# Two blocks instead of one in six attention steps: where a transformer kernel computes the gates of its merge

## The reference, cut to what matters

```
h = rmsnorm(x, norm_g)
a_b, a_c, a_x, a_z, c_q, c_kv, k_pe, b_z, dq, dk, dv, c_z, gate_pre = split(h @ w_in)

u = a_c * a_x                                  # branch a: a convolution over 3 tokens
conv = conv_b + sum(shift(u, tap) * conv_w[tap] for tap in range(3))
y_a = a_b * conv * silu(a_z)
y_b = causal_attention(q, k, v) * silu(b_z)    # branch b: 8 heads (MLA)
y_c = dilated_attention(dq, dk, dv) * silu(c_z)  # branch c: 8 heads, 3 dilations each

g_a, g_b, g_c = split(sigmoid(gate_pre + b_gate))
merged = g_a * (y_a @ w_out_a) + g_b * (y_b @ w_out_b) + g_c * (y_c @ w_out_c)
return x + merged @ w_o
```

## Time and profile before

| | us |
|---|---|
| median of 3 runs | 1566.07 |
| lowest and highest run | 1561.93, 1566.72 |
| the profiled execution, its own time | 1560.04 |
| its span, first to last instruction | 1558.2 |
| TensorE busy | 1503.1 |
| VectorE busy | 1025.5 |
| ScalarE busy | 854.6 |
| GpSimd busy | 83.9 |
| mean granted TensorE clock | 0.993 |

### The profile page before, as it was taken

How to read it: one execution, slowest core, us unless ns; L and a number is a source line. 1 busy time by engine, 2 the same in 40 slices (tenths; PEclk the granted TensorE clock), 3 DMA queues, 4 the chain that set the end, 5 groups by cost and what they waited for, 6 DMA issues and landing times.

```text
span 1558.2 us, 31924 instructions
## 1 busy us (share of the span) xinstructions
PE 1503.1 (96%) x11856; PEld 1411.6 (91%) x11856; DVE 1025.5 (66%) x1774; ACT 854.6 (55%) x1433; POOL 83.9 (5%) x136
## 2 busy tenths in 40 slices
PE   8988999999999999999999999899999999989998
PEld 7777999999989899999999988789999898878998
DVE  2787788898955556555467647775646664776664
ACT  3446566544445646664466755554446675655453
POOL 0111000111000000000000000310000000031000
PEclk9999999999999999999999999999999999999999
DMA  9775488898663355666463553226546355413663
GB/s 375 265 259 183 150 299 290 287 386 315 234 206 119 95 186 165 192 195 191 149 222 123 161 178 123 69 96 189 187 153 206 120 168 171 142 55 98 197 194 122
DMA packets 81341, 292.78 MB, mean 188 GB/s; under 512 B 9200, under 2 KB 10480, under 8 KB 81088
## 3 DMA queue, kind: packets, MB, share of 16 engines
q1 hardware_dynamic: 67408, 244.03, 47.7%
q0 software_dynamic: 11792, 42.83, 8.0%
q10 hardware_dynamic: 2016, 4.21, 0.8%
HBM read 289.99 MB, written 1.05 MB: 187 GB/s over the span
## 4 chain that ended last, share of the span: by engine, by line
PE 47%; issue 40%; DVE 6%; ACT 3%; POOL 2%; DMA 1%; SPq 0%; POOLq 0%; DVEq 0%; ACTq 0%
PE G L450 12%; PE G L451 12%; PE G L452 12%; POOL bias L426 2%; DVE wlo L1374 2%; DVE aw L1382 1%; ACT whi L968 1%; PE S L531 1%; PE G L476 1%; PE G L478 1%; PE G L477 1%; PE Tp L758 1%; PE G L496 1%; PE G L502 1%; PE Tp L557 0%
## 5 line engine op out<-in xcount | busy, mean ns | idle before, releaser
L1374 DVE TENSOR_TENSOR wlo<-raw,whi 128x1024 fp32r<-128x1024 f32 x444 | 541.9, 1223 | 317.0 <-ACT whi L968 310.8
L450 PE MATMUL G<-h,whi 128*128 128x256 f32 x2192 | 626.2, 286 | 5.5 <-DVE cz L1825 3.6
L451 PE MATMUL G<-h,whi 128*128 128x256 f32 x2192 | 610.9, 279 | 0.0
L452 PE MATMUL G<-h,wlo 128*128 128x256 f32 x2192 | 610.6, 279 | 0.0
L968 ACT ACTIVATE whi<-raw 128x1024 fp32r<-128x1024 f32 x444 | 468.9, 1058 | 232.6 <-PE G L452 180.2
L450 PEld LDWEIGHTS G<-h,whi 128*128 128x128 f32 x2192 | 415.8, 190 | 15.7 <-issue 12.1
L451 PEld LDWEIGHTS G<-h,whi 128*128 128x128 f32 x2192 | 414.5, 189 | 1.8 <-issue 0.5
L452 PEld LDWEIGHTS G<-h,wlo 128*128 128x128 f32 x2192 | 414.0, 189 | 0.0
L1382 DVE CUSTOM_DVE_ANT_0 aw<-aw,cs,cols 128x1024 f32<-128x1024 f32 x80 | 102.3, 1278 | 0.0
L450 PE MATMUL G<-ah,whi 128*128 128x256 f32 x352 | 97.2, 276 | 0.0
L451 PE MATMUL G<-ah,whi 128*128 128x256 f32 x352 | 97.2, 276 | 0.0
(11 more groups left out here) (290 smaller groups left out, 2300.9 us busy)
## 6 DMA issues: line engine op xcount, KB each, us to landing
raw<-in_w SPq DMA_DIRECT2D x444, 512.0 KB, 4.1
aw<-in_ada POOLq DMA_DIRECT2D x80, 512.0 KB, 5.1
adaw<-in_ada SPq DMA_DIRECT2D x8, 1024.0 KB, 17.8
sn<-in_uq ACTq DMA_DIRECT2D x2, 768.0 KB, 6.9
x<-in_x SPq DMA_DIRECT2D x1, 1024.0 KB, 5.5
pt<-in_ukv ACTq DMA_DIRECT2D x2, 512.0 KB, 8.5
out<-x SPq DMA_DIRECT2D x4, 256.0 KB, 2.4
dist<-in_dist POOLq DMA_DIRECT2D x1, 576.0 KB, 4.1
```

What stands on the lines that cost most here:

```text
L450: pe.matmul(o, wh, mv[:, 0:T], start=(k == 0), stop=False)
L451: pe.matmul(o, wh, mv[:, T:2 * T], start=False, stop=False)
L452: ins = pe.matmul(o, wl, mv[:, 0:T], start=False, stop=(k == k_of - 1))
L1374: dve.tensor_tensor(wlo[:, s, :], raw[:, s, :], whi[:, s, :], ALU.subtract).then_inc(w_lo, 1)
```

## The change

Six gate blocks a layer, those of mm = 1 (`EARLY`), leave the merge. Each of the steps 9 to 14 gets one, behind its convolution block. A table `WHAT` now says of every block beside the heads what it is ("z", "conv" or "gate") and its number; a table `MERGE` gives the first block and tile of each round of the merge, and the rounds of mm = 1 consist of their `w_out` block alone. ScalarE takes the tanh of an early gate tile in `head_block` and puts it in `sq` instead of `th`, where it stays until VectorE multiplies by it in mm = 1. VectorE does nothing for a gate block in the steps but `next_lo`. Blocks, tiles, instructions and bytes are the same in number; the weights are laid out in the new order.

```diff
-H_MERGE = 64
+H_MERGE = 70
...
-for _n in range(H_MERGE - H_CZ):
-    BESIDE[0 if _n < 3 else _n - 2 if _n < 18 else 16].append(H_CZ + _n)
+WHAT = {}
+EARLY = 1
+for _n in range(20):
+    _i = 0 if _n < 3 else _n - 2 if _n < 18 else 16
+    for _w in [("z", _n) if _n < 4 else ("conv", _n - 4)] + ([("gate", _i - 9)] if 9 <= _i < 15 else []):
+        WHAT[H_CZ + len(WHAT)] = _w
+        BESIDE[_i].append(H_CZ + len(WHAT) - 1)
+assert len(WHAT) == H_MERGE - H_CZ
+
+
+MERGE = {}
+_b = _g = H_MERGE
+for _n in range(12):
+    MERGE[_n // 3, _n % 3] = (_b, _g)
+    _b, _g = (_b + 1, _g + 2) if _n // 3 == EARLY else (_b + 3, _g + 4)
+H_WO_TILE = _g
...
-                        bb, n = B_HYB + H_MERGE + 9 * mm + 3 * r, G_HYB + H_MERGE + 12 * mm + 4 * r
-                        run(bb, n, 1, 8, of_h, b4=b4, g4=g4)
-                        if mm == 0 and r == 0:
-                            pair_outs(7)
-                        run(bb + 1, n + 1, 1, 8, of_h, b4=b4, g4=g4)
-                        if mm == 0 and r == 0:
-                            pe.wait_ge(y_lo, l * 12 + 12)
-                        run(bb + 2, n + 2, 2, 4, lambda m, k: yh[:, 4 * ((2 * r + m) % 3) + k, :], b4=b4, g4=g4,
+                        bb, n = B_HYB + MERGE[mm, r][0], G_HYB + MERGE[mm, r][1]
+                        if mm != EARLY:
+                            run(bb, n, 1, 8, of_h, b4=b4, g4=g4)
+                            if mm == 0 and r == 0:
+                                pair_outs(7)
+                            run(bb + 1, n + 1, 1, 8, of_h, b4=b4, g4=g4)
+                            if mm == 0 and r == 0:
+                                pe.wait_ge(y_lo, l * 12 + 12)
+                            bb, n = bb + 2, n + 2
+                        run(bb, n, 2, 4, lambda m, k: yh[:, 4 * ((2 * r + m) % 3) + k, :], b4=b4, g4=g4,
                             half=half_done)
...
+                def gate_tanh(dst, mm, pair, n):
+
+                    col = 8 * (pair % 3) + 2 * mm + pair // 3
+                    freed(act.activation(dst[:, pair, :], gslot(G_HYB + n), ACT.Tanh, scale=0.5,
+                                         bias=hb[:, col:col + 1]), n)
+
                 def head_block(j):
                     done(j)
-                    t, kind = (j - H_A) // 4, (j - H_A) % 4
-                    if j < H_A:
-                        act.activation(cz[:, j - H_CZ, :], gslot(G_HYB + j), ACT.Tanh, scale=0.5).then_inc(tanh_ready, 1)
+                    what, n = WHAT[j]
+                    t, kind = n // 4, n % 4
+                    if what == "z":
+                        act.activation(cz[:, n, :], gslot(G_HYB + j), ACT.Tanh, scale=0.5).then_inc(tanh_ready, 1)
+                    elif what == "gate":
+                        gate_tanh(sq, EARLY, n, j)
...
+                def merged(m):
+                    act.wait_ge(m_ready, l * 8 + m + 1)
+                    act.activation(mh[:, m, 0:T], mg[:, m % 2, :], ACT.Copy, scale=0.5).then_inc(m_hi, 1)
+
                 for mm in range(4):
-                    for q in range(9):
-                        j = H_MERGE + 9 * mm + q
+                    for r in range(3):
+                        j, n = MERGE[mm, r]
+                        for q in range(0 if mm == EARLY else 2):
+                            done(j)
+                            gate_tanh(th, mm, 2 * r + q, n + q)
+                            next_hi(j)
+                            if r == 2 and q == 0:
+                                merged(2 * mm)
+                            j += 1
                         done(j)
-                        if q % 3 < 2:
-                            pair = 2 * (q // 3) + q % 3
-                            n = H_MERGE + 12 * mm + 4 * (q // 3) + q % 3
-                            col = 8 * (pair % 3) + 2 * mm + pair // 3
-                            freed(act.activation(th[:, pair, :], gslot(G_HYB + n), ACT.Tanh, scale=0.5,
-                                                 bias=hb[:, col:col + 1]), n)
                         next_hi(j)
-                        if q in (6, 8):
-                            m = 2 * mm + q // 8
-                            act.wait_ge(m_ready, l * 8 + m + 1)
-                            act.activation(mh[:, m, 0:T], mg[:, m % 2, :], ACT.Copy, scale=0.5).then_inc(m_hi, 1)
+                        if r == 1 and mm == EARLY:
+                            merged(2 * mm)
+                    merged(2 * mm + 1)
...
-                    if j < H_A:
-                        dve.wait_ge(tanh_ready, l * 12 + (4 + j - H_CZ + 1))
-                        freed(dve.scalar_tensor_tensor(out=cz[:, j - H_CZ, :], in0=cz[:, j - H_CZ, :], scalar=1.0,
+                    what, t = WHAT[j]
+                    if what == "z":
+                        dve.wait_ge(tanh_ready, l * 12 + (4 + t + 1))
+                        freed(dve.scalar_tensor_tensor(out=cz[:, t, :], in0=cz[:, t, :], scalar=1.0,
                                                        in1=gslot(n), op0=ALU.add, op1=ALU.mult), j)
+                    if what != "conv":
                         next_lo(j)
                         return
...
-                        bb = H_MERGE + 9 * mm + 3 * r
-                        gate = G_HYB + H_MERGE + 12 * mm + 4 * r + q % 2
-                        n = gate + 2
+                        bb, n = MERGE[mm, r][0], G_HYB + MERGE[mm, r][1] + q % 2
                         m = 2 * mm + q // 3
-                        next_lo(bb + q % 2)
+                        if mm == EARLY:
+                            gate, tg = G_HYB + [j for j in WHAT if WHAT[j] == ("gate", q)][0], sq
+                        else:
+                            gate, tg = n, th
+                            next_lo(bb + q % 2)
+                            bb, n = bb + 2, n + 2
                         if q % 2:
-                            done(bb + 2)
+                            done(bb)
                         else:
                             dve.wait_ge(half_done, l * 12 + 3 * mm + r + 1)
                         dve.wait_ge(slot_free[gate % 4], taken(gate) + g4)
...
-                            freed(dve.scalar_tensor_tensor(out=th[:, q, :], in0=th[:, q, :], scalar=1.0, in1=gslot(n),
+                            freed(dve.scalar_tensor_tensor(out=tg[:, q, :], in0=tg[:, q, :], scalar=1.0, in1=gslot(n),
                                                            op0=ALU.add, op1=ALU.mult), n - G_HYB)
...
-                            next_lo(bb + 2)
+                            next_lo(bb)
```

More of the change, by code:

```diff
@@ L1332, in _ @@
                         for j in TAKEN[i]:
-                            if j >= H_A and (j - H_A) % 4 == 3:
-                                t = (j - H_A) // 4
+                            if WHAT[j][0] == "conv" and WHAT[j][1] % 4 == 3:
+                                t = WHAT[j][1] // 4
                                 y_split(t, (a_ready, l * 4 + t + 1), at[:, 3, :])
@@ L1822, in head_block @@
                     n = G_HYB + j
-                    if j < H_A:
-                        dve.wait_ge(tanh_ready, l * 12 + (4 + j - H_CZ + 1))
-                        freed(dve.scalar_tensor_tensor(out=cz[:, j - H_CZ, :], in0=cz[:, j - H_CZ, :], scalar=1.0,
+                    what, t = WHAT[j]
+                    if what == "z":
+                        dve.wait_ge(tanh_ready, l * 12 + (4 + t + 1))
+                        freed(dve.scalar_tensor_tensor(out=cz[:, t, :], in0=cz[:, t, :], scalar=1.0,
                                                        in1=gslot(n), op0=ALU.add, op1=ALU.mult), j)
+                    if what != "conv":
                         next_lo(j)
                         return
-                    t, kind = (j - H_A) // 4, (j - H_A) % 4
+                    t, kind = t // 4, t % 4
                     if kind == 1:
@@ L1871, in _ @@
                         for j in TAKEN[i]:
-                            if j >= H_A and (j - H_A) % 4 == 3:
-                                y_split((j - H_A) // 4, at[:, 3, :])
+                            if WHAT[j][0] == "conv" and WHAT[j][1] % 4 == 3:
+                                y_split(WHAT[j][1] // 4, at[:, 3, :])
                     if i >= 3 and i % 2:
@@ L1891, in _ @@
                         if q % 3 == 0:
-                            freed(dve.scalar_tensor_tensor(out=mg[:, m % 2, :], in0=th[:, q, :], scalar=1.0, in1=gslot(n),
+                            freed(dve.scalar_tensor_tensor(out=mg[:, m % 2, :], in0=tg[:, q, :], scalar=1.0, in1=gslot(n),
                                                            op0=ALU.add, op1=ALU.mult), n - G_HYB)
                         else:
-                            freed(dve.scalar_tensor_tensor(out=th[:, q, :], in0=th[:, q, :], scalar=1.0, in1=gslot(n),
+                            freed(dve.scalar_tensor_tensor(out=tg[:, q, :], in0=tg[:, q, :], scalar=1.0, in1=gslot(n),
                                                            op0=ALU.add, op1=ALU.mult), n - G_HYB)
```

(12 more changed lines are left out.)

4 lines of the change are left out of this document (2 added, 2 removed).

## The result

The changed kernel takes 1596.24 us (median of 4 runs, 1594.04 to 1609.03), the kernel before in the same measurement 1566.05 us (4 runs, 1561.93 to 1566.72): a ratio of 1.0201, 95% interval 1.0163 to 1.0239. In a second measurement it was 1600.03 against 1567.35 us, 1.0191 (1.0147 to 1.0235). So it is slower by about 30 us; 1592 was predicted.

The account below looks back on a forecast made before the run. TensorE, busy 1503 of 1558 us, was taken as the bound. Per layer, steps +24.1, merge -15.7 and clock +5.1 gave +13.5, both layers +27.0 us: 1592 us, range 1574 to 1608.

Parts of the forecast that it names:

- The tile wait: Steps 9 to 14: blocks wait for a G tile VectorE frees late; new idling 16.1 us a layer.
- Step 9: First step with an added block: its gate block waits for step 8's kind-2 tile; length 10.8 us, +1.7 on 9.04.
- The steps in sum: Steps 9 to 14 together: +24.1 us a layer for work and waits, before the clock's +5.1.
- The clock: Slow starts of TensorE behind the idles of steps 10, 12 and 14: 1.7 us each, +5.1 us a layer.
- HAM oscillation: Skill section on repeating waits that each drop the clock: all three idles of both layers start slow; without it 10.2 us less.
- the rival in which the clock stays up: Steps 9 to 14: the wait is there without slow starts, 5.1 us a layer less, 1583 us; chance 0.2.
- Step 15: Step behind the six changed ones: keeps its blocks, has no late tile, adds 0.
- My cover for the lo: Steps 9 to 14: VectorE's added lo (1.22 us a step) costs nothing; if cover failed, 7 us a layer.
- The merge: Six gate blocks fewer save 16.9 us a layer, dense mm = 1 rounds give back 1.2: -15.7 a layer.
- The first rival: Steps 9 to 14: added blocks simply fill TensorE's idle time, -15 us in all, 1551 us; chance 0.05.

Follow-up runs that it names:

- the filler: The changed kernel with eleven multiplications of a tile of ones behind the scores in steps 10, 12 and 14, to keep TensorE busy: 1588.21 us, ratio 1.0122 to before.
- the early release: The changed kernel with VectorE's operations on a step's convolution tiles put ahead of the minima: 1556.8 us, ratio 0.9936 to the kernel before.
- the pair first: The changed kernel with only the product of a pair (hpair) moved ahead of the lo parts in odd steps: 1602.93 us, ratio 1.0231 to before.
- the plain swap: The changed kernel with a step's gate block ahead of its convolution block, VectorE following the same order: 1582.33 us, ratio 1.0095 to the kernel before.

## Why the prediction was right

It predicted 1592 (1574 to 1608), +27.0 us; the medians differ by 30.2, the traces from step 8 on by 29.4.

- **The tile wait** was the deciding step, and came as worked out: 1.8, 4.1, 0, 4.1, 2.0, 4.1 us predicted for steps 9 to 14, and 1.82, 4.05, 0, 4.05, 1.95, 4.05 measured. Taking away the late release alone turns +29.4 into -9.4 us. Steps without a slow start are the predicted 12.9 (step 13 here 12.94, steps 10 and 12 with the filler 12.74 and 12.93), and step 11 is the predicted 10.9.
- **Step 9** had a misread start. The row of before in the earlier trace rows that begins at 974.74 was cut by my own window: TensorE's first scores of that step begin at 973.86, so that before it took 9.92 us and not 9.04. I carried the cut through, so the added 1.7 us was right (11.70 - 9.92 = 1.78) and the length of 10.8 wrong by the same 0.9. A stretch has to begin at a row of the timeline.
- **The steps in sum**: 50.07 us before, with that start, 79.73 after, +29.7 a layer in both layers (79.70 - 49.94 in the second), of which 24.1 for work and waits and 5.1 for the clock were predicted, 29.2.
- **The clock**: 1.7 us for each of three idles, 5.1; what steps 10, 12 and 14 take above 12.9 is 2.6 + 1.4 + 1.5 = 5.5, and in the second profiled execution 1.2 + 2.4 + 1.4 + 1.3 = 6.3 with step 13. The sum is near, but two errors of size cancel in it. A short stretch cost less than 1.7 us, because part of it lay in the wait, and one of the three was long and cost more: the low clock of step 10 held from 994.6 to 1001.4, and TensorE went on only at 995.80. The rule of the Trainium skill ("TensorE: Matmul & The Clock Gate", "HAM oscillation") agrees here: every 4.05 us idle of both layers was followed by a start at 0.50. Keeping TensorE busy took 8 us off the changed kernel by its first median and 12 by its second, and some 5 and 10 by the traces from step 8 on, and the rival in which the clock stays up (1583) falls with it.
- **Step 15 was not 0.** It waits 1.74 us in layer 1 and 1.00 in layer 2, where before it waited 0.69 and 0.25, because the lo of the sixth gate block stands ahead of hpair. My cover for the lo, idle time of VectorE, counted the engine's share and not what is queued behind the instruction: the rule that I had applied to the tile, and not to the lo.
- **The merge**: the waits of 0.68 and 0.46 us in the dense rounds are the predicted 0.7 and 0.5. From the scores of step 15 to those of the next step 8, or the end, the time fell by 16.4 us in layer 1 (337.54 to 321.13) and 13.6 in layer 2 (141.67 to 128.04), 30.0 together. The predicted 31.4, less the 1.1 and 0.8 us by which step 15's wait grew, is 29.6. That the sum comes out is luck in part. The price of 2.82 us a block was read from a stretch in which TensorE ran at the slower of two paces, both at granted clock 1.00. In 20 us without idle time the view counts 173 matmuls in the merge of layer 1 before, and 179 in that of layer 2 before and in that of layer 1 after, here in this order:

```profile
1060.00:1080.00 20.00, 20.00 (x173) 20.00 (x172) 11.78 (x16) 9.96 (x14) 0.00 (x0) 1.00 0.61 191
1480.00:1500.00 20.00, 20.00 (x179) 20.00 (x178) 13.09 (x19) 10.31 (x14) 0.00 (x0) 1.00 0.62 197
```

```profile
1080.00:1100.00 20.00, 20.00 (x179) 20.00 (x178) 11.94 (x17) 10.95 (x16) 0.00 (x0) 1.00 0.62 194
```

The mean distance from one start to the next is 0.1178 us in the first of these merges and 0.1134 to 0.1138 in the others and in that of layer 2 after. At 0.1134 six blocks are 16.3 us and not 16.9, and the 30 blocks that stay in layer 1 took 30 x 24 x 0.004 = 2.9 us less by the pace and not by the change, about the 2.8 by which the two layers differ. What sets the pace is open.

- **The first rival** (the idle time simply filled, 1551) had chance 0.05 for the change as it is. It is what the early release makes of it: 1556.8.

## What to carry to other kernels

When a block is added between others, ask who frees the tile that it writes, and what stands ahead of that operation on its engine: here 39 us (1596 to 1557) hung on where VectorE does one 0.4 us operation, and moving it ahead of the minima turned a loss of 2% into a gain of 0.6%. Idle time of an engine covers an added instruction only if nothing that others wait for is queued behind it. A short wait of TensorE can cost more than its length through the clock, so test the two prices apart, one kernel that frees the tile and one that only keeps TensorE busy.

## What the runs showed of the chip

Whether the clock falls behind an idle is not told by its length alone. Idles of 4.05 us were followed by 0.50 in all eighteen cases (two profiled executions of the changed kernel, one of the version with the pair first). Of the eight idles of 1.94 or 1.95 us in step 13 six were followed by it: none in the first profile of the changed kernel, both in its second, in that of the filler and in that of the pair first. With the plain swap five idles of 2.16 to 2.25 us were, and one of 2.25 us (step 10 of layer 1) was not. The idle of 1.8 us in step 1, behind the cz tile, was in eight of twenty cases, over the ten profiled executions and both layers. The idle of 2.87 us in the earlier trace rows was not, but in the changed kernel the same wait of the same code (2.88 us, up to 151.95) was, with a granted clock of 0.51 from 151.50 to 154.80; and the wait of the earlier trace rows that a slow stretch followed at 543.50 had none behind it there (2.49 us, up to 548.18). The slow stretch lasted about 3.4 or 6.8 us, and which of several idles got the long one changed between two executions of the same kernel.

The two executions of the changed kernel also differed by 11.25 us before its first dilated step, and most of this is TensorE's pace at granted clock 1.00. Here are 20 us of the same dense part, in the first profile and then in the second, with 179 and 172 matmuls:

```profile
620.00:640.00 20.00, 20.00 (x179) 20.00 (x178) 11.99 (x16) 12.49 (x18) 0.00 (x0) 1.00 0.64 191
```

```profile
620.00:640.00 20.00, 20.00 (x172) 20.00 (x171) 11.70 (x15) 12.07 (x17) 0.00 (x0) 1.00 0.58 184
```

Ahead of step 8 the mean distance between the starts of its dense matmuls into G is 0.1141 us in the first and 0.1164 in the second, over some 5640 of them 13 us; the second has 3.4 us less at clock 0.50, which gives 1.7 back. The pace changes within an execution, in all kernels here, and no run here shows why. So a difference of a few us between two single traces is not yet a difference between two kernels; the medians over many runs are what the verdicts above rest on.
